# HGRN heads by tokens: scores as the stationary operand, squares summed on ScalarE, three transposes back to channels

## The chip, the cores and the metric

The program runs on one NeuronCore of a Trainium2 chip. The metric is the device time of one execution in microseconds (us); smaller is better. In this text PE is TensorE, DVE is VectorE, ACT is ScalarE, and POOL is GpSimd.

## The reference

One inference step of a two-layer trunk: layer 0 mixes tokens with an mLSTM, layer 1 with HGRN2, and each mixer is followed by a SwiGLU block. There are 256 prompt tokens and 8 sampled sequences of 8 tokens, so 320 tokens in all. The change touches only the HGRN2 mixer, whose core is, for each of 16 heads with 128 key channels and 128 value channels:

```python
def body(S, xs):
    qc, kc, lfc, ic = xs
    A = jnp.cumsum(lfc, axis=1)
    diff = jnp.where(causal[None, :, :, None, None], A[:, :, None] - A[:, None, :], -jnp.inf)
    wd = jnp.exp(diff)
    s = jnp.einsum('bthc,bjhc,btjhc->btjh', qc, kc, wd)
    oc = jnp.einsum('btjh,bjhv->bthv', s, ic) + jnp.einsum('bthc,bhcv->bthv', qc * jnp.exp(A), S)
    A_last = A[:, -1]
    S_new = jnp.exp(A_last)[..., None] * S + jnp.einsum('bjhc,bjhv->bhcv', kc * jnp.exp(A_last[:, None] - A), ic)
    return S_new, oc
...
o = rms_norm(from_chunks(os_), gn_g.reshape(H_HEADS, H_DV)).reshape(B, T, H_HEADS * H_DV)
out = (o * jax.nn.silu(g)) @ w_out.astype(jnp.float32)
```

The root mean square of `rms_norm` is taken for each token over the 128 value channels of a head.

## The kernel before

The activations are kept turned, channels on the 128 partitions and the 320 tokens along the free axis. Every weight matrix is read in tiles of 128 output columns by up to 16 blocks `k` of 128 rows. SP loads a tile (1 MB) into a ring of four slots `raw`. ACT copies it to `w_hi` in a rounded format (`split_high`, two halves), DVE subtracts to get the remainder `w_lo` (`split_low`, two halves), and PE makes three products for each k: hi by hi, hi by lo, lo by hi (`products`, lines 390 to 392), 48 products for a tile, each with 320 moving columns. `hi_done` counts ACT's halves, `lo_done` DVE's, `gemm_done` PE's tiles. Each engine has a program of its own in a fixed order written out by hand; semaphores alone tie them together.

The HGRN stage (`H_IN`) is a loop over 16 heads, four weight tiles a head: f, q, i, g. The work of a head is spread over three turns of the loop. In turn `it` PE makes the tiles of head `it`, and between them it does what belongs to the heads `one_back` and `two_back`:

- after tile 0: `h8(two_back)`, a product with a matrix of ones that sums the squares of the head's output over the channels (and spreads the sum over all partitions), and `turn_values(one_back)`, six transposes and one product;
- after tile 1: `by_columns(one_back)`, the many small products that give the scores, and last the old states' part of the sampled tokens, `OLD`;
- after tile 2: `h7(one_back)`, the head's outputs into `MX[5]` (bank 7), five products with the values `i_tok` as the stationary operand and the scores moving; the fifth adds `OLD`, which ACT copied to `hold_tok`. Then the products for the new states.

ACT squares the output (`h8`) when `h7` of PE is done (`g_o`), and in the next turn takes Ln and Exp of the sum (`h9`), which gives the reciprocal root `h_rs` of 128 by 320. DVE multiplies output, root and gate in `h9`, two passes, and `h10` of ACT and DVE round the result to `g_hi` and `g_lo`. At the end of each turn DVE copies the new prompt state (`prompt_S`), updates the eight sampled states (`sample_S`), and then makes `split_low` of the next head's tile 0, `h4` and `h5` (the keys and queries with their decays, up to `k_last` with `g_keys` at line 1379).

After the loop, the last two heads are finished within the first two tiles of the output projection `H_OUT` (`last_heads`): PE does `h8(14)` and `turn_values(15)` within tile 0, `by_columns(15)` within tile 1, then `h7(15)` and `h8(15)`, waits for `g_gated`, and makes the last two k of both tiles. Tile 2 of `H_OUT` is split by ACT only after the last states have been stored (`S_stored`).

Of the kernel before, what the change touches and what calls it, by code (L numbers as in the profile page):

```python
# [19 lines left out]
P = 128  # L20
D = 2048
KT = D // P
TP = 256
NB, TB = 8, 8
TS = NB * TB
T = TP + TS
# [3 lines left out]
HH = 16  # L30
# [65 lines left out]
def trunk(nc, x_prompt, x_sample, C_in, n_in, m_in, S_in, norm_mix_g, norm_ffn_g, norm_final_g,  # L96
# [7 lines left out]
    with ExitStack() as ctx:  # L104
# [148 lines left out]
        scores = carve(T)  # L253
# [8 lines left out]
        h_sq, h_rs = carve(T), carve(T)  # L262
        h_y = h_sq
        after_levels = Carve(at_pairs)
        i_half, hk_tok, hold_tok = after_levels(2 * P), after_levels(3, P), after_levels(P)
# [16 lines left out]
        I_TURNED, K_TURNED, OLD = bank[2][:, 0:3 * P], bank[3][:, 0:3 * P], bank[6][:, 3 * P:4 * P]  # L282
# [49 lines left out]
        g_gsig = sem("g_gsig")  # L332
# [4 lines left out]
        g_ikept, g_kkept, g_ihalf, g_o, g_sq, g_sum, g_rstd = (sem("g_" + n) for n in ("ikept", "kkept", "ihalf", "o", "sq", "sum", "rstd"))  # L337
# [287 lines left out]
        def _(act):  # L625
# [215 lines left out]
            def h7(h):  # L841
                act.wait_ge(g_levels, h + 1)
                act.activation(hold_tok, OLD, ACT.Copy)
                act.activation(hk_tok, K_TURNED.rearrange("p (a b) -> p a b", a=3), ACT.Copy).then_inc(g_kkept, 1)

            def h8(h):
                act.wait_ge(g_o, h + 1)
                act.activation(h_sq, MX[5][:, 0:T], ACT.Square).then_inc(g_sq, 1)

            def h9(h):  # L850
                act.wait_ge(g_sum, h + 1)
                act.activation(h_rs, MX[4][:, 0:T], ACT.Ln, scale=1.0 / P, bias=eps_col[:, :])
                act.drain()
                act.activation(h_rs, h_rs, ACT.Exp, scale=-0.5).then_inc(g_rstd, 1)
# [6 lines left out]
            def h_body(it, one_back, two_back):  # L861
# [10 lines left out]
                if two_back is not None:  # L872
                    h9(two_back)
# [19 lines left out]
            def h_end():  # L893
# [3 lines left out]
                h9(HH - 2)  # L897
# [6 lines left out]
                h9(HH - 1)  # L904
# [23 lines left out]
        def _(dve):  # L928
# [402 lines left out]
            def spread_near():  # L1331
# [7 lines left out]
                dve.copy_predicated(scores[:, TP:T].rearrange("p (j c) -> p j c", j=2), own_group[:, 0:2, :],  # L1339
                                    scores_near[:, 64:].rearrange("p (j c) -> p j c", j=1).to_broadcast((P, 2, 32)))  # L1340
# [76 lines left out]

            def h9(h):
                dve.wait_ge(g_rstd, h + 1)
                dve.tensor_tensor(h_y, MX[5][:, 0:T], h_rs, ALU.mult)  # L1420
                dve.drain()
                dve.tensor_tensor(h_y, h_y, gate, ALU.mult).then_inc(g_full, 1)
# [6 lines left out]
            def h_body(it, one_back, two_back):  # L1429
# [28 lines left out]
                if one_back is not None:  # L1458
                    prompt_S(one_back)
                    sample_S(one_back)  # L1460
                split_low(dve, H_IN, it + 1, 0)
# [13 lines left out]
            def h_end():  # L1475
# [10 lines left out]
                prompt_S(HH - 1)  # L1486
                h9(HH - 1)
# [17 lines left out]
        def _(pe):  # L1505
# [81 lines left out]

            picked = ident[:, :].rearrange("p (g r) -> p g r", g=4)[:, :, 0:PICKED]
# [165 lines left out]
            def h7(h):  # L1754
# [14 lines left out]
            def h8(h):  # L1769
                pe.wait_ge(g_sq, h + 1)  # L1770
                pe.wait_ge(g_Sp, h + 1)
                pe.matmul(MX[4][:, 0:T], ones[:, :], h_sq, start=True, stop=True).then_inc(g_sum, 1)  # L1772

            def h_body(it, one_back, two_back):
# [8 lines left out]
                if two_back is not None:  # L1783
                    pe.wait_ge(g_rstd, two_back + 1)
# [70 lines left out]
```

## Time and profile before

| | us |
|---|---|
| median of 3 runs | 3136.4 (3136.33, 3136.4, 3138.96) |
| profiled execution, its own time | 3136.22 |
| its span | 3134.7 |
| PE busy | 3082.4 (98%) |
| DVE busy | 1791.6 (57%) |
| ACT busy | 1169.5 (37%) |

The span is what the profile shows of the execution; what lies around it is 1.5 us. The busy time of an engine is the union of its instructions. The fp32 products that are not in the rounded format appear as two PE instructions each (two passes), the transposes as one.

### The profile page before, as it was taken

The page shows a single profiled execution, that of the slowest core. Times are in us where ns is not written, and L with a number is a line of the kernel's source. Part 1 is how long each engine was busy: PE and PEld are TensorE (multiplying, and loading weights), DVE is VectorE, ACT ScalarE, POOL GpSimd, SP SyncE. Part 2 cuts the span into 40 slices and gives each one's busy share as a digit, 9 for nine tenths or more (in the row PEclk, how much of TensorE's full clock was granted, in tenths as well). Part 3 has the DMA queues.
Part 4 walks back from the last instruction along what each step waited for, and adds up shares of the span by engine and source line. Part 5 has one row for each costly group of instructions (what it writes and reads, how often), then busy time and mean ns, then how long its engine had stood idle before and what let it go on. Part 6 is the DMA issues. An engine that isn't in the chain of part 4 may idle for free.

```text
span 3134.7 us, 58211 instructions
## 1 busy us (share of the span) xinstructions
PE 3082.4 (98%) x23124; PEld 3037.3 (97%) x23124; DVE 1791.6 (57%) x3128; ACT 1169.5 (37%) x1658; POOL 74.4 (2%) x132
## 2 busy tenths in 40 slices
PE   7999999999999999999999999989999999999998
PEld 6999989999999999999999999989999999999997
DVE  6666665555445544555687888755555345544554
ACT  4433333333223332334455555534333233322333
POOL 2000000000000000000000000000000000000000
PEclk9999999999999999999999999989999999999999
DMA  6564636555555555555555565545555555555543
GB/s 158 149 190 136 191 111 184 146 152 147 148 148 148 151 154 150 148 141 141 159 159 160 141 167 156 149 127 150 148 147 150 153 145 153 149 149 148 147 134 114
DMA packets 856561, 470.15 MB, mean 150 GB/s; under 512 B 10424, under 2 KB 846144, under 8 KB 856480
## 3 DMA queue, kind: packets, MB, share of 16 engines
q1 hardware_dynamic: 844080, 433.09, 50.2%
q0 software_dynamic: 10144, 35.74, 3.7%
q8 instruction: 57, 0.93, 0.1%
q10 hardware_dynamic: 2256, 0.19, 0.1%
q14 instruction: 24, 0.20, 0.0%
HBM read 447.46 MB, written 21.53 MB: 150 GB/s over the span
## 4 chain that ended last, share of the span: by engine, by line
PE 97%; DVE 1%; DMA 1%; ACT 0%; issue 0%; DVEq 0%; ACTq 0%; POOL 0%; POOLq 0%
PE bank L390 31%; PE bank L392 30%; PE bank L391 30%; PE bank L1718 1%; DMA arena<-in_mlstm_w_in_dram 0%; PE bank L1766 0%; PE bank L1772 0%; PE bank L1610 0%; PE bank L1764 0%; PE bank L1561 0%; PE bank L1599 0%; PE bank L1750 0%; PE bank L1592 0%; PE bank L1630 0%; DVE w_lo L380 0%
## 5 line engine op out<-in xcount | busy, mean ns | idle before, releaser
L390 PE MATMUL bank<-h_hi,w_hi 128*128 128x320 f32 x4608 | 1433.5, 311 | 5.8 <-DVE w_lo L380 4.9
L391 PE MATMUL bank<-h_lo,w_hi 128*128 128x320 f32 x4608 | 1424.5, 309 | 0.1
L392 PE MATMUL bank<-h_hi,w_lo 128*128 128x320 f32 x4608 | 1424.5, 309 | 0.0
L373 ACT ACTIVATE w_hi<-raw 128x1024 fp32r<-128x1024 f32 (+1 forms) x832 | 818.8, 1032 | 778.1 <-PE bank L392 774.6
L380 DVE TENSOR_TENSOR w_lo<-raw,w_hi 128x1024 fp32r<-128x1024 f32 (+1 forms) x832 | 963.3, 1199 | 199.3 <-ACT w_hi L373 198.6
L390 PEld LDWEIGHTS bank<-h_hi,w_hi 128*128 128x128 f32 x4608 | 865.8, 188 | 22.7 <-issue 16.6
L391 PEld LDWEIGHTS bank<-h_lo,w_hi 128*128 128x128 f32 x4608 | 866.0, 188 | 1.6 <-issue 1.3
L392 PEld LDWEIGHTS bank<-h_hi,w_lo 128*128 128x128 f32 x4608 | 865.7, 188 | 0.0
L390 PE MATMUL bank<-g_hi,w_hi 128*128 128x320 f32 x1920 | 598.5, 312 | 14.0 <-DVE w_lo L380 6.4
L391 PE MATMUL bank<-g_lo,w_hi 128*128 128x320 f32 x1920 | 596.2, 311 | 0.0
L392 PE MATMUL bank<-g_hi,w_lo 128*128 128x320 f32 x1920 | 596.2, 310 | 0.0
L1054 DVE TENSOR_TENSOR arena<-bank,rstd 128x320 f32<-128x320 f32 (+1 forms) x296 | 133.6, 460 | 532.0 <-PE bank L392 515.4
L390 PEld LDWEIGHTS bank<-g_hi,w_hi 128*128 128x128 f32 x1920 | 363.2, 189 | 16.3 <-DVE w_lo L380 7.3
L391 PEld LDWEIGHTS bank<-g_lo,w_hi 128*128 128x128 f32 x1920 | 363.3, 189 | 0.0
L392 PEld LDWEIGHTS bank<-g_hi,w_lo 128*128 128x128 f32 x1920 | 363.1, 189 | 0.0
L1212 DVE TENSOR_TENSOR x<-x,bank 128x320 f32 (+1 forms) x128 | 62.3, 487 | 316.1 <-PE bank L392 316.0
L782 ACT ACTIVATE arena<-arena 128x320 f32<-128x320 f32 x88 | 41.5, 472 | 482.3 <-DVEq L1248 482.3
L413 ACT ACTIVATE h_hi<-x,gains (+1 forms) x48 | 27.0, 563 | 189.7 <-DVEq L1217 182.3
L423 DVE SCALAR_TENSOR_TENSOR h_lo<-x,gains,h_hi (+1 forms) x48 | 26.5, 552 | 53.2 <-ACT h_hi L413 53.2
L1254 DVE TENSOR_TENSOR g_hi<-arena 128x320 f32 (+1 forms) x88 | 43.3, 493 | 14.7 <-issue 13.8
L1258 DVE TENSOR_TENSOR g_lo<-arena,g_hi 128x320 f32 (+1 forms) x88 | 43.3, 492 | 12.5 <-issue 11.6
L417 ACT ACTIVATE arena<-x 128x320 f32 (+1 forms) x64 | 29.4, 459 | 54.8 <-DVEq L1217 54.8
(318 smaller groups left out, 1446.8 us busy)
## 6 DMA issues: line engine op xcount, KB each, us to landing
raw<-in_ffn_w_up_dram SPq DMA_DIRECT2D x176, 1024.0 KB, 5.7
raw<-in_ffn_w_down_dram SPq DMA_DIRECT2D x64, 1024.0 KB, 5.8
raw<-in_hgrn_w_in_dram SPq DMA_DIRECT2D x64, 1024.0 KB, 6.3
raw<-in_mlstm_w_in_dram SPq DMA_DIRECT2D x48, 1024.0 KB, 6.1
raw<-in_ffn_w_down_dram SPq DMA_DIRECT2D x32, 768.0 KB, 5.0
raw<-in_mlstm_w_out_dram SPq DMA_DIRECT2D x16, 1024.0 KB, 6.0
raw<-in_hgrn_w_out_dram SPq DMA_DIRECT2D x16, 1024.0 KB, 5.8
raw<-in_state_mlstm_C_dram POOLq DMA_DIRECT2D x8, 1024.0 KB, 9.1
```

The lines of the kernel that those rows point to most:

```text
L373: act.activation(w_hi[:, s % 2, part], raw[:, s % ph.ring, part], ACT.Copy).then_inc(hi_done, 1)
L380: dve.tensor_tensor(w_lo[:, s % 2, part], raw[:, s % ph.ring, part], w_hi[:, s % 2, part].bitcast(F32), ALU.subtract).then_inc(lo_done, 1)
L390: pe.matmul(out, tile_hi, hi[:, k, :], start=(k == 0), stop=False)
L391: pe.matmul(out, tile_hi, lo[:, k, :], start=False, stop=False)
L392: last = pe.matmul(out, tile_lo, hi[:, k, :], start=False, stop=(k == ph.k - 1))
L417: act.activation(square[:, parity, :], x[:, bass.ds(j, 1), :], ACT.Square).then_inc(x_sq_done, 1)
L782: act.activation(f_sig[:, (s - 1) // 2, :], fa[:, (s - 1) // 2, :], ACT.Sigmoid).then_inc(f_sig_done, 1)
L1054: return dve.tensor_tensor(out, src, rstd[:, cols], ALU.mult)
L1212: add = dve.tensor_tensor(x[:, bass.ds(j, 1), :], x[:, bass.ds(j, 1), :], bank[s % ph.banks][:, 0:T].rearrange("p (a t) -> p a t", a=1), A ...
L1254: dve.tensor_tensor(g_hi[:, bass.ds(pair, 1), :], f_sig[:, u:u + 1, :], fu.rearrange("p (a t) -> p a t", a=1), ALU.mult)
L1258: dve.tensor_tensor(g_lo[:, bass.ds(pair, 1), :], f_full[:, u:u + 1, :], g_hi[:, bass.ds(pair, 1), :].bitcast(F32), ALU.subtract).then_inc ...
L1718: last = pe.matmul(LEVEL[li][group(j), 32 * b:32 * b + 32], left[:, c], right[:, c], start=True, stop=True)
```

## The change

The outputs are made with tokens on the partitions: in PE's `h7` the scores are now the stationary operand and the values move. `OLD` is written straight into the third block of the output bank, so the fifth product, ACT's copy to `hold_tok` and that buffer are gone; the sampled tokens' scores are laid out in 128 columns instead of 64, with the 64 tokens in groups of 16. ACT squares each of three blocks of 128 by 128 and sums it along the free axis into one word (`accum_out`), and takes Ln and Exp of 128 by 3 words in the same turn; DVE scales the three blocks by them (`scale_out`) into `o_tok`. PE turns the three blocks back to channels in place of the product with ones, the third with the columns of the identity permuted so that the tokens come out in order. DVE's `h9` multiplies only by the gate. PE no longer waits for `g_rstd` ahead of `by_columns`.

```diff
-        scores = carve(T)
+        scores = carve(TP + P)
...
-        I_TURNED, K_TURNED, OLD = bank[2][:, 0:3 * P], bank[3][:, 0:3 * P], bank[6][:, 3 * P:4 * P]
+        I_TURNED, K_TURNED, OLD = bank[2][:, 0:3 * P], bank[3][:, 0:3 * P], bank[7][:, 2 * P:3 * P]
...
             def h7(h):
                 act.wait_ge(g_levels, h + 1)
-                act.activation(hold_tok, OLD, ACT.Copy)
                 act.activation(hk_tok, K_TURNED.rearrange("p (a b) -> p a b", a=3), ACT.Copy).then_inc(g_kkept, 1)
 
             def h8(h):
                 act.wait_ge(g_o, h + 1)
-                act.activation(h_sq, MX[5][:, 0:T], ACT.Square).then_inc(g_sq, 1)
-
-            def h9(h):
-                act.wait_ge(g_sum, h + 1)
-                act.activation(h_rs, MX[4][:, 0:T], ACT.Ln, scale=1.0 / P, bias=eps_col[:, :])
+                for b in range(3):
+                    act.activation(o_tok[:, b, :], MX[5][:, b * P:(b + 1) * P], ACT.Square, accum_out=o_sums[:, b:b + 1])
                 act.drain()
-                act.activation(h_rs, h_rs, ACT.Exp, scale=-0.5).then_inc(g_rstd, 1)
+                act.activation(o_rs, o_sums, ACT.Ln, scale=1.0 / P, bias=eps_col[:, :])
+                act.drain()
+                act.activation(o_rs, o_rs, ACT.Exp, scale=-0.5).then_inc(g_rstd, 1)
...
+            def scale_out(h):
+                dve.wait_ge(g_rstd, h + 1)
+                dve.tensor_tensor(o_tok, MX[5][:, 0:3 * P].rearrange("p (b c) -> p b c", b=3),
+                                  o_rs.rearrange("p (b c) -> p b c", c=1).to_broadcast((P, 3, P)), ALU.mult).then_inc(g_scaled, 1)
+
             def h9(h):
-                dve.wait_ge(g_rstd, h + 1)
-                dve.tensor_tensor(h_y, MX[5][:, 0:T], h_rs, ALU.mult)
-                dve.drain()
-                dve.tensor_tensor(h_y, h_y, gate, ALU.mult).then_inc(g_full, 1)
+                dve.wait_ge(g_oturned, h + 1)
+                dve.tensor_tensor(h_y, MX[4][:, 0:T], gate, ALU.mult).then_inc(g_full, 1)
...
                     prompt_S(one_back)
                     sample_S(one_back)
+                    scale_out(one_back)
                 split_low(dve, H_IN, it + 1, 0)
                 h4(it)
...
-                pe.matmul(out[:, 0:P], i_tok[:, 0, :], scores[:, 0:P], start=True, stop=True, skip_group_check=True)
-                pe.matmul(out[:, P:TP], i_tok[:, 1, :], scores[:, P:TP], start=False, stop=True, skip_group_check=True)
-                pe.matmul(out[:, P:TP], i_tok[:, 0, :], scores_far, start=False, stop=True, skip_group_check=True)
-                pe.matmul(out[:, TP:T], i_tok[:, 2, :], scores[:, TP:T], start=False, stop=True, skip_group_check=True)
-                pe.matmul(out[:, TP:T], hold_tok, picked, start=False, stop=True, skip_group_check=True)
+                pe.matmul(out[:, 0:P], scores[:, 0:P], i_tok[:, 0, :], start=False, stop=True, skip_group_check=True)
+                pe.matmul(out[:, P:TP], scores[:, P:TP], i_tok[:, 1, :], start=False, stop=False, skip_group_check=True)
+                pe.matmul(out[:, P:TP], scores_far, i_tok[:, 0, :], start=False, stop=True, skip_group_check=True)
+                pe.matmul(out[:, TP:TP + P], scores[:, TP:], i_tok[:, 2, :], start=False, stop=True, skip_group_check=True)
...
             def h8(h):
-                pe.wait_ge(g_sq, h + 1)
+                pe.wait_ge(g_scaled, h + 1)
                 pe.wait_ge(g_Sp, h + 1)
-                pe.matmul(MX[4][:, 0:T], ones[:, :], h_sq, start=True, stop=True).then_inc(g_sum, 1)
+                for b in range(2):
+                    pe.transpose(MX[4][:, b * P:(b + 1) * P], o_tok[:, b, :], ident[:, :])
+                pe.transpose(MX[4][:, TP:TP + P].rearrange("p (u g r) -> p u g r", u=2, g=4), o_tok[:, 2, :], picked_first).then_inc(g_oturned, 1)
```

PE's program between tile 0 and the six transposes of `turn_values`, in the loop's body, before (L1772 is the product with ones, L1725 the first of `turn_values`):

```order
L392 MATMUL bank<-h_hi,w_lo 128x320
L1770 REGISTER_ALU
L1772 MATMUL bank<-arena,ones 128x320 [waits g_Sp,g_sq]
L1722 ISA
L1725 MATMUL bank<-ident,arena 128x128 [waits g_S,evac_done]
```

and with the change (its L1728 is the line that was L1725):

```order
L392 MATMUL bank<-h_hi,w_lo 128x320
L1772 REGISTER_ALU
L1775 MATMUL bank<-ident,arena 128x128 [waits g_Sp,g_scaled]
L1775 MATMUL bank<-ident,arena 128x128
L1776 MATMUL bank<-ident,arena 128x128
L1725 ISA
L1728 MATMUL bank<-ident,arena 128x128 [waits g_S,evac_done]
```

One product of 320 columns became three transposes of 128 columns, and it waits for a result of DVE instead of one of ACT.

PE's `h7` in the loop's body before, with the two products for the prompt state (L1764) behind it:

```order
L1758 MATMUL bank<-arena 128x128 [waits g_kkept,g_ihalf,g_full]
L1759 MATMUL bank<-arena 128x128
L1760 MATMUL bank<-arena 128x128
L1761 MATMUL bank<-arena 128x64
L1762 MATMUL bank<-ident,arena 128x64
L1764 MATMUL bank<-arena 128x128 x2
```

and with the change:

```order
L1761 MATMUL bank<-arena 128x128 [waits g_kkept,g_ihalf,g_full]
L1762 MATMUL bank<-arena 128x128
L1763 MATMUL bank<-arena 128x128
L1764 MATMUL bank<-arena 128x128
L1766 MATMUL bank<-arena 128x128 x2
```

Two products of 64 columns became one of 128; the waits are the same.

DVE's program at the end of a turn before, from `sample_S` (L1414) to the split of the next head's tile 0 (L380):

```order
L1407 COPY arena<-bank 128x128 [waits S_stored]
L1414 SCALAR_TENSOR_TENSOR arena<-arena,bank 128x128 x8
L379 ISA
L380 TENSOR_TENSOR w_lo<-raw,w_hi 128x1024 [waits hi_done]
```

and with the change:

```order
L1402 COPY arena<-bank 128x128 [waits S_stored]
L1409 SCALAR_TENSOR_TENSOR arena<-arena,bank 128x128 x8
L1417 TENSOR_TENSOR arena<-bank,arena 128x384 [waits g_rstd]
L379 ISA
L380 TENSOR_TENSOR w_lo<-raw,w_hi 128x1024 [waits hi_done]
```

`scale_out`, with its wait for ACT, now stands ahead of the split; its own two passes in `h9` became one.

## Rows read from the trace of the kernel before

**Rows 1.** The page, busy time, share of the span, instructions:

```profile
PE 3082.4 (98%) x23124; PEld 3037.3 (97%) x23124; DVE 1791.6 (57%) x3128; ACT 1169.5 (37%) x1658; POOL 74.4 (2%) x132
```

**Rows 2.** Windows, one turn of the loop; PEclk is the granted clock:

```profile
core 0: us, PE busy (x) PEld busy (x) DVE busy (x) ACT busy (x) POOL busy (x), PEclk, DMA share, GB/s
1781.00:1815.15 34.15, 34.15 (x370) 33.10 (x369) 27.52 (x73) 17.84 (x34) 2.34 (x3) 1.00 0.56 155
```

**Rows 3.** Timeline of PE between tiles 0 and 1 (start us, length us):

```profile
1780.85 0.70 PE L1772 MATMUL bank<-arena,ones 128*128 128x320 f32 x2
1781.39 0.49 PE L1725 MATMUL bank<-ident,arena 128*128 128x128 f32 x3
1781.72 0.49 PE L1728 MATMUL bank<-ident,arena 128*128 128x128 f32 x3
...
1782.42 0.31 PE L391 MATMUL bank<-h_lo,w_hi 128*128 128x320 f32 x1
```

**Rows 4.** Timeline of PE, start of tile 2 and `h7`:

```profile
1791.38 0.41 PE L390 MATMUL bank<-h_hi,w_hi 128*128 128x320 f32 x1
...
1798.53 0.38 PE L1758 MATMUL bank<-arena 128*128 128x128 f32 x2
...
1799.19 0.33 PE L1761 MATMUL bank<-arena 128*128 128x64 f32 x2
1799.36 0.39 PE L1762 MATMUL bank<-ident,arena 128*128 128x64 f32 x2
1799.58 0.66 PE L1764 MATMUL bank<-arena 128*128 128x128 f32 x4
```

**Rows 5.** Timeline of PE's weight loads in the same `h7`:

```profile
1799.08 0.30 PEld L1761 LDWEIGHTS bank<-arena 128*128 128x128 f32 x2
1799.30 0.30 PEld L1762 LDWEIGHTS bank<-ident,arena 128*128 128x128 f32 x2
1799.53 0.53 PEld L1764 LDWEIGHTS bank<-arena 128*128 128x128 f32 x4
```

**Rows 6.** Line 1728, transposes of `turn_values`, duration min/median/max in ns:

```profile
L1728 PE MATMUL bank<-ident,arena x48: 272/273/328, 1541.3 to 2050.8; 128*128 128x128 f32 x48
```

**Rows 7.** Timeline of DVE, end of a turn and the next turn's first split:

```profile
1801.26 2.15 DVE L1414 SCALAR_TENSOR_TENSOR arena<-arena,bank 128x128 f32<-128x128 f32 x8
1803.32 2.35 DVE L380 TENSOR_TENSOR w_lo<-raw,w_hi 128x1024 fp32r<-128x1024 f32 x2
...
1813.77 2.35 DVE L380 TENSOR_TENSOR w_lo<-raw,w_hi 128x1024 fp32r<-128x1024 f32 x2
```

**Rows 8.** Timeline of ACT, reads of a bank in the loop:

```profile
1791.51 0.28 ACT L843 ACTIVATE arena<-bank 128x128 f32<-128x128 f32 x1 [3.19 <-PE bank L1750]
1791.68 0.49 ACT L844 ACTIVATE arena<-bank 128x384 f32<-128x384 f32 x1
...
1800.96 0.44 ACT L848 ACTIVATE arena<-bank 128x320 f32<-128x320 f32 x1 [5.11 <-PE bank L1766]
```

**Rows 9.** Timeline of ACT, a square's sum being read out at the start:

```profile
30.22 0.20 ACT L649 ACTIVATION_READ_ACCUMULATOR g_lo<-arena 64x1 f32 x1
30.32 0.52 ACT L637 ACTIVATE h_hi<-bank,gains 128x320 fp32r<-128x320 f32 x1
```

**Rows 10.** Groups of ACT's instructions in the last 16 us (count, busy us, mean ns):

```profile
L916 ACT ACTIVATE rstd_cols<-bank,eps_col 128x2 f32<-128x2 f32 (+1 forms) x2 | 0.4, 254 | 0.0
L919 ACT ACTIVATE rstd_cols<-rstd_cols 128x2 f32<-128x2 f32 (+1 forms) x2 | 0.3, 194 | 0.1
```

**Rows 11.** Waits of PE from 2030 to 2090 us (total us, times, longest):

```profile
PE bank L390 <- DVE w_lo L380: 6.4, 1, 6.4
PE bank L390 <- DVE g_lo L1426: 3.4, 1, 3.4
PE bank L1758 <- DVE arena L1401: 1.2, 1, 1.2
PE bank L1772 <- ACT arena L848: 0.6, 1, 0.6
PE bank L1728 <- DVE arena L1379: 0.3, 1, 0.3
```

**Rows 12.** Timelines of PE, DVE and ACT behind the last `h7`:

```profile
2050.52 0.55 PE L1728 MATMUL bank<-ident,arena 128*128 128x128 f32 x3 [0.25 <-DVE arena L1379]
...
2067.46 0.44 ACT L848 ACTIVATE arena<-bank 128x320 f32<-128x320 f32 x1 [6.74 <-PE bank L1766]
...
2070.45 0.49 DVE L1422 TENSOR_TENSOR arena<-arena 128x320 f32<-128x320 f32 x1
```

**Rows 13.** Windows around PE's restart at tile 2 of `H_OUT`:

```profile
2084.00:2086.00 2.00, 2.00 (x9) 2.00 (x8) 1.28 (x3) 2.00 (x4) 0.00 (x0) 0.50 0.55 144
2088.00:2090.00 2.00, 2.00 (x16) 2.00 (x15) 0.03 (x1) 0.00 (x0) 0.00 (x0) 1.00 0.44 104
```

More of the change, by code:

```diff
@@ L261, in trunk @@
         gate = carve(T)
-        h_sq, h_rs = carve(T), carve(T)
-        h_y = h_sq
+        h_y, o_tok = carve(T), carve(3, P)
+        o_sums, o_rs = carve(3), carve(3)
         after_levels = Carve(at_pairs)
-        i_half, hk_tok, hold_tok = after_levels(2 * P), after_levels(3, P), after_levels(P)
+        i_half, hk_tok = after_levels(2 * P), after_levels(3, P)
         assert after_levels.at <= at_pairs + sum(level_width(l) for l in LEVELS)
@@ L329, in trunk @@
         n_turned, n_done, n_stored = sem("n_turned"), sem("n_done"), sem("n_stored")
-        g_gsig = sem("g_gsig")
+        g_gsig, g_scaled = sem("g_gsig"), sem("g_scaled")
         g_fsig, g_f, g_logf = sem("g_fsig"), sem("g_f"), sem("g_logf")
@@ L336, in trunk @@
         g_pair, g_keys, g_turned, g_levels = sem("g_pair"), sem("g_keys"), sem("g_turned"), sem("g_levels")
-        g_ikept, g_kkept, g_ihalf, g_o, g_sq, g_sum, g_rstd = (sem("g_" + n) for n in ("ikept", "kkept", "ihalf", "o", "sq", "sum", "rstd"))
+        g_ikept, g_kkept, g_ihalf, g_o, g_rstd, g_oturned = (sem("g_" + n) for n in ("ikept", "kkept", "ihalf", "o", "rstd", "oturned"))
         g_Sp = sem("g_Sp")
@@ L871, in h_body @@
                     h6(one_back)
-                if two_back is not None:
-                    h9(two_back)
                 split_high(act, H_IN, it, 2)
@@ L896, in h_end @@
                 h6(HH - 1)
-                h9(HH - 2)
                 act.wait_ge(evac_done, H_IN.end)
@@ L903, in h_end @@
                 h8(HH - 1)
-                h9(HH - 1)
                 h10(HH - 1)
@@ L1338, in spread_near @@
                                     scores_near[:, 0:64].rearrange("p (b j c) -> p b j c", b=2, j=1).to_broadcast(shape))
-                dve.copy_predicated(scores[:, TP:T].rearrange("p (j c) -> p j c", j=2), own_group[:, 0:2, :],
-                                    scores_near[:, 64:].rearrange("p (j c) -> p j c", j=1).to_broadcast((P, 2, 32)))
+                dve.copy_predicated(scores[:, TP:].rearrange("p (j u w) -> p j u w", j=2, u=2)[:, :, :, 0:PICKED],
+                                    own_group[:, 0:2, :].rearrange("p j (u r) -> p j u r", u=2),
+                                    scores_near[:, 64:].rearrange("p (j u r) -> p j u r", j=1, u=2).to_broadcast((P, 2, 2, PICKED)))
             def h3(h):
@@ L1486, in h_end @@
                 prompt_S(HH - 1)
+                scale_out(HH - 1)
                 h9(HH - 1)
@@ L1586, in m4 @@
                 pe.matmul(MX[0][:, TP + P:TP + P + TS], kT[:, TP:TW], qT[:, TP:T], start=True, stop=True).then_inc(m_scores, 1)
+            picked_first = ident[:, :].rearrange("p (g u r) -> p u g r", g=4, u=2)
             picked = ident[:, :].rearrange("p (g r) -> p g r", g=4)[:, :, 0:PICKED]
@@ L1782, in h_body @@
                 products(pe, H_IN, it, 1, h_hi, h_lo)
-                if two_back is not None:
-                    pe.wait_ge(g_rstd, two_back + 1)
                 if one_back is not None:
@@ L1806, in last_heads @@
                 if at == (1, 6):
-                    pe.wait_ge(g_rstd, HH - 1)
                     by_columns(HH - 1)
```

## The prediction

> **What bounds the kernel now.** I read the page first: PE is busy 98% of the span, DVE 57%, ACT 37% [rows 1]. The windows of the HGRN loop come next. One turn takes 34.15 us, PE is busy for all of it at full clock, DVE for 27.52 and ACT for 17.84 [rows 2], and the waits of PE over seven turns in a row list nothing. So inside the loop a change of PE's own instructions shows in the time one for one, and work on DVE or ACT is free until it is late for PE. Behind the loop it is the other way round: PE waits there for 0.3, 1.2, 0.6, 3.4 and 6.4 us [rows 11], and the chain through ACT and DVE counts. The kernel is therefore summed in two parts: the loop, up to the moment at which head 14's `h7` is done (`g_o`), by PE's instructions; behind that, by the chain.
>
> **Part one, the product with ones becomes three transposes.** The timeline gives starts, and in a stream it is the distance of starts that costs. From L1772 to L1725 there are 0.54 us (two passes of 320 columns, 0.27 each). From the first L1725 to the first L1728 there are 0.33 us for three transposes, 0.11 each, with other transposes behind them [rows 3]. The new instructions have that shape and stand right ahead of these. To L391 at 1782.42 the stretch from L1725 is 1.03 us, so nothing is hidden at its end. I take 0.54 - 0.33 = 0.21 off, and 0.20 because the seven loads ahead of tile 1 go at 0.11 each and the first may not be covered by a long product any more. The third transpose reads the identity in another order; the fifth product of `h7` reads it in pieces of 16 already and shows the pace of its neighbours (0.22 for two passes, 1799.36 to 1799.58 [rows 4]), so I give that nothing. Bounds: 0.22 saved; or, if each transpose costs its recorded duration of 273 ns [rows 6], 0.82 - 0.54 = 0.28 lost.
>
> **Part two, `h7`.** Moving columns are 128+128+128+64+64 = 512 before and 4 x 128 = 512 after, so by columns nothing is saved. But the two products of 64 columns do not cost half: from 1799.19 to 1799.58 they take 0.39 us, while the three of 128 ahead of them take 0.66, 0.22 each [rows 4]. The reason stands in the weight loads: a pair of passes starts its loads every 0.22 us, whatever the columns (1799.08, 1799.30, 1799.53 [rows 5]). One stationary operand less, with two loads, is 0.22. From the starts of the products it is 0.39 - 0.22 = 0.17. I take 0.22, since the loads set the pace and the product at L1764 can start no earlier than its own load; bounds 0 and 0.22. Changing which operand is stationary costs nothing by these rows: both are 128x128 words.
>
> The Trainium skill ("TensorE: Matmul & The Clock Gate", Part 2, "LDWEIGHTS (loading the stationary operand)") says that a load lasts its number of columns over 1.2 GHz, 107 ns for 128, whatever the rows; the trace agrees with 0.11 us of pitch, and by it two loads less are 0.21 in place of 0.22.
>
> **Sum of the loop.** `h7` of heads 0 to 14 lies ahead of the cut: 15 x 0.22 = 3.3 us. `h8` of heads 0 to 13 too: 14 x 0.20 = 2.8. Together 6.1 us less.
>
> **What the loop hides.** ACT's copy to `hold_tok` goes (0.17 of pitch [rows 8]); it had no reader that was late. ACT's `h8` grows. A square of 128x128 from a bank is 0.28 long and 0.17 in pitch [rows 8], and each sum is read out by an instruction of 0.20, 0.10 in pitch [rows 9]: three are 3 x 0.27 + 0.10 = 0.91 us, at most 3 x 0.48 = 1.44. Ln and Exp of three words are like the small ones at the end, 0.25 and 0.19 [rows 10], with some 0.07 for each drain: 1.49 in all, 2.1 at most. From 1800.96 [rows 8] the root is there at 1802.5, or 1803.1. DVE comes to `scale_out` when `sample_S` is done, at 1803.3 [rows 7]: it does not wait. `scale_out` is 384 columns from a bank; at 0.49 for 320 [rows 12] that is 0.58 long, and since successive passes overlap by about 0.1, 0.47 of delay. Behind it on DVE stand the split of the next tile 0, `h4`, `h5` and the split of tile 1. Tile 0's first half is ready at 1803.32 + 1.14 = 1804.5, later 1804.9; PE needs it when tile 3 ends, some 7.1 us before L1772 of the next turn, which starts at 1780.85 + 34.15 = 1815.0 (a tile lasts 1798.53 - 1791.38 = 7.15 [rows 4]), so at 1807.9: 3 us in hand. Tile 1's first half is ready at 1813.77 + 1.14 = 1814.9 [rows 7], later 1815.4; PE starts tile 1 one product before the L391 of [rows 3] plus 34.15, at 1816.4, and 0.2 sooner by the shorter `h8`: 0.8 us in hand. This is the thinnest cover of the change: 0.47 of 1.5 us is used. ACT starts its split of tile 0 one us later and still feeds DVE in time (first half done 1803.5). DVE gives the 0.4 back when `h9` makes one pass in place of two. The removed wait of PE for `g_rstd` was not felt, and its removal is worth nothing.
>
> **Part three, the end.** Counted from `g_o` of head 14, DVE is 0.47 later at `g_keys`, for which PE already waits 0.25 us [rows 11, 12], because in `last_heads` only five k stand in place of a whole tile. So the 0.20 that `h8(14)` saves turns into waiting, and the rest of the chain (`by_columns(15)`, then DVE's level work, for which PE waits 1.2) moves by +0.47. `h7(15)` gives 0.22 back. Then the last output: from ACT's square at 2067.46 to the end of DVE's second pass at 2070.45 + 0.49 = 2070.94 there are 3.48 us [rows 12]. In their place: ACT 1.49, DVE 0.58, three transposes after a wait 0.55 [rows 12], DVE's gate 0.49, and 0.03 for each of three hand-overs: 3.20, so -0.28 (up to +0.3 with the dear squares). The rounding to `g_hi`, `g_lo`, the states and their store behind it are unchanged. Net: +0.47 - 0.22 - 0.28 = 0.0.
>
> **Total:** -6.1 us. Against the profiled execution, 3136.22, that is 3130.1; against the median of the runs shown, 3136.4, which lies 0.2 above it, 3130.3. I give **3130.2 us**. What a measurement of this kernel can tell from no change is about 0.2%, 6.3 us, so the forecast sits right at that bound, just inside "no change".
>
> [...] The trace shows the transposes of `turn_values` at a pitch of 0.11 us inside a turn whose clock is granted in full [rows 2, 3]. [...]
>
> **Rivals.**
> - *Transposes in series.* Each costs its duration [rows 6]: +0.28 x 14 = +3.9 in the loop, -3.3 from `h7`: 3136.9. Against it is the pitch of six of them [rows 3]; for it only that no transposes follow a product of the rounded format now. 4 in 100.
> - *Columns, not loads, set `h7`.* The new fourth product costs 0.39 with what it replaces: only 2.8 is saved, 3133.4. The 0.22 of load pitch speaks against it. With the half-way case of 0.17 (3131.0), 14 in 100 lie between 3131.0 and 3133.6.
> - *PE's clock behind the loop.* After its 6.4 us wait PE runs at 1.2 GHz (0.50 in the windows at 2084) and is back at 2.4 GHz by 2088 [rows 13]; nine products in 2 us there against sixteen later. These some 6 us cost about 2.6. Since all of it now comes 6 us sooner, the clock may come back sooner or later after the restart: I allow -1.5 to +1.5, 3128.7 or 3131.7. 8 in 100 for each side beyond the forecast's own range.
> - *Slower: the root is late for DVE, and DVE for tile 1.* `scale_out` waits for ACT ahead of the split, so a late root holds DVE, and PE pays once the cover of 1.5 us is used. Each turn already has 0.42 to give. To end over 3142.7 the wait of PE has to be 0.42 + 0.45 = 0.87 in each of 14 turns, so DVE has to be late by about 1.3 + 0.87 = 2.1 us in place of 0.47; the root would then come at about 1805, four us after `g_o`, against an upper bound of 2.1. With twice the bound, 3143. 5 in 100.
>
> **How the numbers follow.** The forecast, 3129.2 to 3131.0, has 58 in 100; the series 4, the columns 14, the clock 8 and 8, the slower one 5, and 3 remain for what I do not see. The range from 3127.4 to 3133.6 leaves out the series, the slower case, the rest and a little of the clock. Faster by over 0.2% means below 3130.1: half of the forecast's case (0.29), the sooner clock (0.08), and what I do not see (0.03), together 0.40. Slower by over 0.2% is the last rival, 0.05. The other half of the forecast, the series, the columns and the later clock stay within: 0.55.
>
> **What the profile would show.** A turn of 33.73 us in place of 34.15, with PE busy throughout; three new transposes with starts 0.11 apart; four pairs of passes in `h7` 0.22 apart; no wait of DVE at `scale_out`; PE's wait for `g_keys` of head 15 grown from 0.3 to about 0.9; the wait ahead of the last products about as before. Wrong would be: a wait of PE on `w_lo` inside the loop, a pitch of the transposes above 0.15, or a last output that takes over a us more.

## The result and the profile after

| | before | changed |
|---|---|---|
| median, 10 runs each | 3138.46 us (3136.33 to 3139.63) | 3131.27 us (3128.51 to 3135.28) |
| ratio | | 0.9979, 95% interval 0.9970 to 0.9987 |
| profiled execution, own time | 3136.22 us | 3131.71 us |
| its span | 3134.7 us | 3130.1 us |

The kernel became faster by 0.21%, 6.6 us by the ratio, and the interval (4.1 to 9.4 us) excludes no change. It lies right at the 0.2% that the prediction took as the least that can be told from no change. The forecast was 6.2 us less. The medians are 7.2 us apart, the two profiled executions only 4.5; most of that gap stands ahead of the HGRN stage, where the two kernels do the same, and is told below.

The page after, busy time, share and instructions, against [rows 1]:

```profile
PE 3078.0 (98%) x23108; PEld 3035.7 (97%) x23108; DVE 1789.3 (57%) x3128; ACT 1168.5 (37%) x1722; POOL 74.4 (2%) x132
```

PE lost 4.4 us of busy time, and ACT has 64 instructions more (for each of 16 heads two more squares and three readings of sums, less one copy) in the same time. The windows of one turn of the loop after, against [rows 2]:

```profile
core 0: us, PE busy (x) PEld busy (x) DVE busy (x) ACT busy (x) POOL busy (x), PEclk, DMA share, GB/s
1824.08:1857.80 33.72, 33.72 (x376) 32.87 (x371) 27.41 (x72) 17.85 (x38) 2.34 (x3) 1.00 0.57 158
```

A turn takes 33.72 us in place of 34.15, and PE is still busy for all of it. The timeline of PE after, between tiles 0 and 1 (start us, length us), against [rows 3]:

```profile
1814.16 0.38 PE L1775 MATMUL bank<-ident,arena 128*128 128x128 f32 x2
1814.38 0.27 PE L1776 MATMUL bank<-ident,arena 128*128 128x128 f32 x1
1814.49 0.49 PE L1728 MATMUL bank<-ident,arena 128*128 128x128 f32 x3
1814.82 0.49 PE L1731 MATMUL bank<-ident,arena 128*128 128x128 f32 x3
```

The three new transposes take 1814.49 - 1814.16 = 0.33 us, where the product with ones took 0.54. The third one, with the identity in another order, costs 0.11 like the others. The same view at `h7`, against [rows 4]:

```profile
1831.62 0.38 PE L1761 MATMUL bank<-arena 128*128 128x128 f32 x2
1831.84 0.39 PE L1762 MATMUL bank<-arena 128*128 128x128 f32 x2
1832.06 0.39 PE L1763 MATMUL bank<-arena 128*128 128x128 f32 x2
1832.29 0.39 PE L1764 MATMUL bank<-arena 128*128 128x128 f32 x2
1832.51 0.61 PE L1766 MATMUL bank<-arena 128*128 128x128 f32 x4
```

Four products at 0.22 each, 0.89 us, where five took 1.05. The state products behind them last 0.61 where they lasted 0.66: that is the other 0.05 of the 0.22 that the prediction took from the starts of the weight loads. ACT and DVE at the end of the turn, against [rows 7, 8]:

```profile
1833.83 0.28 ACT L848 ACTIVATE arena<-bank 128x128 f32<-128x128 f32 x1 [5.05 <-PE bank L1768]
1834.01 0.20 ACT L848 ACTIVATION_READ_ACCUMULATOR arena<-bank 128x1 f32 x1
...
1834.79 0.30 ACT L850 ACTIVATE arena<-arena,eps_col 128x3 f32<-128x3 f32 x1
1835.15 0.21 ACT L852 ACTIVATE arena<-arena 128x3 f32<-128x3 f32 x1
```

```profile
1834.13 2.15 DVE L1409 SCALAR_TENSOR_TENSOR arena<-arena,bank 128x128 f32<-128x128 f32 x8
1836.19 0.55 DVE L1417 TENSOR_TENSOR arena<-bank,arena 128x384 f32<-128x384 f32 x1
1836.66 2.35 DVE L380 TENSOR_TENSOR w_lo<-raw,w_hi 128x1024 fp32r<-128x1024 f32 x2
```

The root is there at 1835.36, 1.53 us after the first square began (1.49 was reckoned), and DVE comes to `scale_out` (L1417) at 1836.19 without a wait. It delays the split by 0.47. Behind the loop, the waits of PE from 2020 to 2090 us, against [rows 11]:

```profile
PE bank L390 <- DVE w_lo L380: 6.5, 1, 6.5
PE bank L1775 <- DVE arena L1417: 2.2, 1, 2.2
PE bank L390 <- DVE g_lo L1426: 1.7, 1, 1.7
PE bank L1761 <- DVE arena L1396: 1.2, 1, 1.2
PE bank L1731 <- DVE arena L1374: 0.9, 1, 0.9
```

The wait for the keys of head 15 (L1374) is 0.9 us in place of 0.3, as forecast. The product with ones stood between two waits of 0.6 and 3.4; now the transposes stand between 2.2 and 1.7.

From one event to the next, the pair of profiled executions differs like this (us, after less before):

| stretch | before | after | difference |
|---|---|---|---|
| start to the old states' products of head 0 | 1550.57 | 1552.51 | +1.94 |
| to the same of head 1 | 35.15 | 35.16 | 0.0 |
| 13 more turns, to head 14 | 444.34 | 438.71 | -5.63 |
| to ACT's first square of head 14 | 9.97 | 9.75 | -0.22 |
| to PE's restart at tile 2 of the output projection | 42.09 | 42.09 | 0.0 |
| to the end of the span | 1052.6 | 1051.9 | -0.7 |

The first and the last row can't be put down to the change. Both kernels do the same work ahead of head 0's old states' products and behind the restart, and a second profiled execution of the same changed kernel (run a2, below) has 1552.7 us in the first row and 1052.8 in the last, which is 0.2 more than before; its row of 42.09 and its steady turn of 33.72 are the same. The first two turns vary as well: together they take 69.65 us before and 69.93 in e10, a variant of before with an edit behind the loop only, and 69.28 and 68.62 in the two executions of the changed kernel.

### The profile page after: what moved, and what is told of

Its sections match the earlier page's. It is cut to its first block, busy times and chain, and to the rows that moved or that the text cites. A ratio compares the mean times of both kernels' runs of the same rounds, so it can differ in the third digit from the quotient of the medians.

```text
span 3130.1 us, 58228 instructions
## 1 busy us (share of the span) xinstructions
PE 3078.0 (98%) x23108; PEld 3035.7 (97%) x23108; DVE 1789.3 (57%) x3128; ACT 1168.5 (37%) x1722; POOL 74.4 (2%) x132
## 4 chain that ended last, share of the span: by engine, by line
PE 97%; DVE 1%; DMA 1%; ACT 0%; issue 0%; DVEq 0%; ACTq 0%; POOL 0%; POOLq 0%
PE bank L390 31%; PE bank L392 30%; PE bank L391 30%; PE bank L1721 1%; DMA arena<-in_mlstm_w_in_dram 0%; PE bank L1768 0%; PE bank L1613 0%; DMA out_dram<-arena 0%; PE bank L1563 0%; PE bank L1602 0%; PE bank L1753 0%; PE bank L1595 0%; PE bank L1766 0%; DVE w_lo L380 0%; PE bank L1633 0%
## 5 line engine op out<-in xcount | busy, mean ns | idle before, releaser
L380 DVE TENSOR_TENSOR w_lo<-raw,w_hi 128x1024 fp32r<-128x1024 f32 (+1 forms) x832 | 964.0, 1201 | 198.5 <-ACT w_hi L373 198.1
L1048 DVE TENSOR_TENSOR arena<-bank,rstd 128x320 f32<-128x320 f32 (+1 forms) x296 | 133.9, 462 | 532.5 <-PE bank L392 515.8
```

The costliest lines, as they stand in the source:

```text
L380: dve.tensor_tensor(w_lo[:, s % 2, part], raw[:, s % ph.ring, part], w_hi[:, s % 2, part].bitcast(F32), ALU.subtract).then_inc(lo_done, 1)
L1048: return dve.tensor_tensor(out, src, rstd[:, cols], ALU.mult)
```

## The experiments

Times of a turn are read from the chain of each profiled execution, as the distance of the same product in two neighbouring turns. Every experiment from e1 to e7 and e11 was run once. These are the rows of the changed kernel (start us, length us), then of e1, e2, e3 and e6:

```profile
1824.08 0.46 PE bank L1753 x15
1857.80 0.46 PE bank L1753 x15
```

```profile
1825.99 0.46 PE bank L1753 x15
1859.93 0.46 PE bank L1753 x15
```

```profile
1823.60 0.46 PE bank L1753 x15
1857.32 0.46 PE bank L1753 x15
```

```profile
1826.53 0.46 PE bank L1753 x15
1860.58 0.46 PE bank L1753 x15
```

```profile
1825.74 0.46 PE bank L1750 x15
1859.65 0.46 PE bank L1750 x15
```

So 33.72, 33.94, 33.72, 34.05 and 33.91 us. The times of one kernel spread over 4.3 us (before, 21 runs) to 6.8 us (changed, 10 runs), so for an effect of 0.2 us a turn it is these rows that decide and not the total.

**e1, one stationary operand more, the same columns.**

```diff
-                pe.matmul(out[:, TP:TP + P], scores[:, TP:], i_tok[:, 2, :], start=False, stop=True, skip_group_check=True)
+                for half in range(2):
+                    c = slice(64 * half, 64 * half + 64)
+                    pe.matmul(out[:, TP + 64 * half:TP + 64 * half + 64], scores[:, TP:], i_tok[:, 2, c], start=False, stop=True, skip_group_check=True)
```

> The changed kernel with the fourth product of h7 made as two of 64 moving columns with the same stationary scores: the same columns, one stationary operand (two loads) more. My theory, that weight loads set the pace of these products at 0.11 us each: a turn of 33.72 + 0.17 to 0.22 = 33.89 to 33.94 us. The rival, that moving columns set it: 33.72.

Measured: 33.94, which is 0.22 more. The moving columns are the same 128, so columns can't be the cause. By their starts the products themselves go from 0.22 to 0.39 us, and the state products behind them from 0.54 to 0.60, as in the kernel before.

**e2, half of the columns, the same stationary operands.**

```diff
-                pe.matmul(out[:, 0:P], scores[:, 0:P], i_tok[:, 0, :], start=False, stop=True, skip_group_check=True)
+                pe.matmul(out[:, 0:64], scores[:, 0:P], i_tok[:, 0, 0:64], start=False, stop=True, skip_group_check=True)
```

and the other three likewise.

> The changed kernel with only the first 64 value channels computed in all four products of h7 (half of the moving columns, the same stationary operands; the outputs of the other channels are left out). Loads set the pace: from the first of the four to the state products still about 0.8 to 0.9 us, a turn of 33.6 to 33.72. Columns set the pace: 0.45 us, a turn of 33.28.

Measured: 33.72, unchanged to the hundredth. The timeline of PE in this run:

```profile
1831.14 0.33 PE L1761 MATMUL bank<-arena 128*128 128x64 f32 x2
1831.31 0.39 PE L1762 MATMUL bank<-arena 128*128 128x64 f32 x2
1831.53 0.39 PE L1763 MATMUL bank<-arena 128*128 128x64 f32 x2
1831.75 0.39 PE L1764 MATMUL bank<-arena 128*128 128x64 f32 x2
1831.98 0.66 PE L1766 MATMUL bank<-arena 128*128 128x128 f32 x4
```

The first pair looks 0.05 shorter by its start, and the state products behind give it back (0.66 in place of 0.61). That is what made the removed pair of the kernel before look like 0.17 in the starts, where 0.22 was saved. The two limits meet near 128 columns: a pass of 320 columns costs 0.27 us [rows 3], so 128 of them are, by an estimate from that row, 0.108 us, and a load is 0.11. Below 128 columns only the load is left, and 64 columns cost what 128 do.

**e3, the transposes as ordinary products.**

```diff
-                    pe.transpose(MX[4][:, b * P:(b + 1) * P], o_tok[:, b, :], ident[:, :])
+                    pe.matmul(MX[4][:, b * P:(b + 1) * P], o_tok[:, b, :], ident[:, :], start=True, stop=True)
```

and the third likewise.

> The changed kernel with the three transposes of h8 made as ordinary products with the identity, two passes each. My theory, that a transpose is one pass at a pitch of 0.11 us and that PE bounds the loop: 0.66 in place of 0.33 us, a turn of 34.05 us, and behind the loop at most 0.3 more. If the transposes went in series with their duration of 0.27, two passes would add 0.8 or more.

Measured: 34.05, 0.33 more: three passes more at 0.11. In these traces a transpose of fp32 words is one pass and a product two, and that is what makes the part pay (0.66 would be dearer than the product with ones, 0.54).

**e6, the two parts apart, on the kernel before.**

```diff
-                pe.matmul(out[:, TP:T], hold_tok, picked, start=False, stop=True, skip_group_check=True)
```

> The kernel before without the fifth product of h7 (the old states' part of the sampled tokens' outputs is left out); ACT's copy of it stays. It separates the two parts of the change: my theory gives h7 0.22 of the 0.43 us of a turn, so 34.15 - 0.22 = 33.93 us here, and the other 0.21 is the transposes' in place of the product with ones. The rival: the removed product is worth its 64 columns in two passes, 0.05, and the rest of the gain came from elsewhere: 34.10.

Measured: 33.91, against 34.15. That product alone is worth 0.24 us a turn. With the 0.21 that the rows give for the transposes (0.54 less 0.33) it makes 0.45, where 0.43 was measured: the two parts add up within 0.02.

**e4 and e5, more work for DVE.** On the changed kernel one pass more of DVE in e4 and three in e5, whose edit is:

```diff
                     scale_out(one_back)
+                    for _ in range(3):
+                        dve.tensor_tensor(h_y, gate, gate, ALU.mult)
+                        dve.drain()
```

> The changed kernel with one more pass of DVE over 320 columns and a drain behind scale_out in the loop, some 0.57 us. By the trace after, tile 1's first half is ready 1.0 us before PE starts tile 1, so no wait: a turn of 33.72 us; behind the loop PE's wait for the keys of head 15 grows from 0.92 to about 1.5 us. The rival, that DVE is already felt by PE: a turn longer by up to 0.57.

> The same with three such passes, some 1.7 us in all, more than the cover of 1.0. PE should wait for the low half of tile 1 by about 0.7 us in each turn: 34.4 us, the whole execution some 10 us longer than the changed kernel (0.7 x 13 and 1.7 less 0 behind the loop). If the cover is larger than I read, less.

e4: a turn from 1824.98 to 1858.70, 33.72 us, so nothing is felt. Behind the loop the wait for the keys grew to 1.22 and not to 1.5: ahead of L1048 behind the loop DVE paused for 0.23 us there where it pauses for 0.61 in the changed kernel, so that pause swallowed some of the delay (more on it under e7). e5: 34.85 us, and 34.86 in the turns behind, so 1.14 more where 0.7 was expected; 3150.9 us in all, 19.6 more than the changed kernel where 10 were expected. From the chain of this run, with PE's wait in the timeline:

```profile
1832.66 1.08 PE bank L1724 x93
1867.51 1.08 PE bank L1724 x93
```

```profile
1824.92 0.41 PE L390 MATMUL bank<-h_hi,w_hi 128*128 128x320 f32 x1 [0.87 <-DVE w_lo L380]
```

The wait is where it was said to be, at the first product of tile 1 for its low half. The profile calls 0.87 us of it a wait; by the starts that product comes 1.25 us behind the one ahead of it (1823.67), in the changed kernel 0.14. It is longer than expected because DVE reaches the split of tile 1 later by 2.04 us and not by 1.7: from the copy of the state to that split it takes 14.92 us (1808.73 to 1823.65), in the changed kernel 12.88 (1833.92 to 1846.80). The three passes and their drains are 1.79 of it, and 0.25 are longer pauses of DVE behind them, for which the profile names no cause. 2.04 - 1.14 gives the cover that was left: 0.90 us, with 0.8 forecast. So `scale_out` used a third of a cover of 1.4 (0.47 + 0.90), and 0.9 us more on DVE before the split of tile 1 would have been free.

**e7 and e11, the delay of the keys behind the loop.** `scale_out` behind the keys, in the loop and for head 14 behind it, and `h8(14)` behind `turn_values(15)`:

```diff
                 dve.tensor_scalar(k_last, k0[:, 0:P], e(2), e(3), ALU.mult, ALU.mult).then_inc(g_keys, 1)
+                if scaled is not None:
+                    scale_out(scaled)
                 pair_diffs(h, 1)
...
-                    scale_out(one_back)
                 split_low(dve, H_IN, it + 1, 0)
...
                 if at == (0, 5):
-                    h8(HH - 2)
                     turn_values(HH - 1)
+                    h8(HH - 2)
```

> The changed kernel with scale_out of DVE moved behind the keys (g_keys) of the next turn, and, for the last heads, PE's turn_values(15) ahead of h8(14). Loop unchanged at 33.72 us a turn. Behind it the wait for the keys of head 15 shrinks again: from ACT's square of head 14 to PE's restart at tile 2 of the output projection 42.09 - 0.47 = 41.6 us. If it was not scale_out that made the keys late there, 42.09.

The loop stayed at 33.72, but the stretch behind it is 42.12 us (2036.77 to 2078.89), not 41.6. The theory that the late keys cost 0.47 there fell as it stood. From ACT's square of head 14 to the end of the keys it is 10.40 us, and 10.90 in the changed kernel. That is 0.50 less, close to the 0.47 that was expected, but it isn't what `scale_out` cost. DVE in the changed kernel, and then in e7:

```profile
2038.96 2.35 DVE L380 TENSOR_TENSOR w_lo<-raw,w_hi 128x1024 fp32r<-128x1024 f32 x2
2045.62 0.49 DVE L1048 TENSOR_TENSOR arena<-bank,rstd 128x320 f32<-128x320 f32 x1 [0.61 <-issue]
```

```profile
2039.45 2.36 DVE L380 TENSOR_TENSOR w_lo<-raw,w_hi 128x1024 fp32r<-128x1024 f32 x2 [0.23 <-ACT w_hi L373]
2045.74 0.49 DVE L1048 TENSOR_TENSOR arena<-bank,rstd 128x320 f32<-128x320 f32 x1 [0.24 <-issue]
```

Counted from the square (2036.13 and 2036.77), the split (L380) starts after 2.83 us in the changed kernel and after 2.68 in e7: only 0.15 sooner, because with `scale_out` out of the way DVE waits for ACT, whose longer `h8` stands ahead of its own half of the split. Another 0.37 comes from the pause ahead of L1048. It is 0.61 us in nine of the profiled executions, and 0.23 or 0.24 in the five (e4, e5, e7, e11, e12) in which DVE's program of the loop was edited; why, no run shows. Before and changed kernel both have the 0.61, so between these two the 0.47 stands: the split starts 2.36 us behind the square before, and 2.83 after.

PE gained nothing from the sooner keys. Its `h8(14)` used to lie in the wait for them, and in e7 it lies behind it and costs its 0.33; what is left, 0.13, went to a wait for the low part of tile 1, of which PE wants both halves here, and for which DVE was as late as before, since `scale_out` now stands between the keys and that split: PE's first product of the tile starts at 2052.30, 0.05 after the end of the split (2049.90 + 2.35). The same 0.05 stands in the changed kernel (2051.70 behind 2049.29 + 2.36) and 0.06 before (2055.14 behind 2052.73 + 2.35), so keys and split hold PE there in one, and to bring the keys alone forward gains nothing. To see whether that reading holds, `scale_out(14)` goes behind the split of tile 1 and `h8(14)` into that tile:

```diff
                 h5(HH - 1)
                 split_low(dve, H_OUT, 0, 1)
+                scale_out(HH - 2)
...
                 if at == (0, 5):
                     turn_values(HH - 1)
+                if at == (1, 3):
+                    h8(HH - 2)
```

> As e7, but behind the loop scale_out(14) stands also behind DVE's split of tile 1 of the output projection, and PE makes h8(14) only at k = 3 of that tile. In e7 the keys came 0.50 us sooner, and nothing was gained, because h8(14), 0.33 us, left PE's waiting time, and by my reading 0.13 more went to a wait for tile 1's low half. So from ACT's square of head 14 to that of head 15: 27.67 - 0.50 + 0.33 = 27.50 us here, 27.63 if tile 1's half was not what held e7.

Measured: 2036.30 to 2063.81, 27.51 us, as expected for the reading that the low part of tile 1 held e7 (27.50). So the edits are worth 0.16 us in all. The keys are as early as in e7, and by the same two parts, so this 0.16 holds for a kernel with the short pause; what the order alone is worth was not measured.

**e8 and e10, the wait of 6.5 us.** The waits of PE show something as large as the change: behind the last output PE waits 6.4 us in both kernels [rows 11], because ACT splits tile 2 only after the states have been stored, and DVE after the residual tile that waits for the same. The edit, for the output projection alone, on ACT and on DVE (on DVE too the splits of tiles 2 and 3 leave their old place):

```diff
-                    if not (ph is H_OUT and s < 2):
+                    if ph is not H_OUT:
                         split_high(act, ph, 0, s)
                     if s in boundary:
                         boundary[s]()
+                    if ph is H_OUT and s in (1, 2):
+                        split_high(act, ph, 0, s + 1)
                     if s == 1 and ph is H_OUT:
                         act.wait_ge(S_stored, HH * 32)
...
                     dve.sem_inc(x_done, 1)
+                    if between:
+                        between()
                     x_tile_dve(dve, r, j, s % 2, isinstance(j, int) and j == 0)
...
+                        early = ph is H_OUT and s < 3
+                        x_evac(ph, r, 0, s - 1, (lambda: split_low(dve, ph, 0, s + 1)) if early else None)
```

> The changed kernel with the splits of tiles 2 and 3 of the output projection made by ACT and DVE ahead of the wait for the stored states instead of behind it. The wait of 6.5 us of PE for w_lo there falls to about 1 us, so 5.5 us less; PE's clock, low from 2068 on, should come back sooner by as much. I expect 3126 us or less beside 3131 for the changed kernel, ratio to the kernel before 0.996. The rival: tile 3 or the residual tiles behind it become late instead, and part of it is given back.

Measured: 3123.18 us (3122.72 to 3125.04, 4 runs), ratio to before 0.9954, interval 0.9938 to 0.9971. The timeline of PE, with its last two waits:

```profile
2065.66 0.64 PE L390 MATMUL bank<-g_hi,w_hi 128*128 128x320 f32 x1 [1.70 <-DVE g_lo L1431]
2070.10 0.64 PE L390 MATMUL bank<-g_hi,w_hi 128*128 128x320 f32 x1 [0.87 <-DVE w_lo L380]
```

and the windows behind it, in which the number behind the six busy times is the granted clock (0.50, then 0.98):

```profile
2070.00:2074.00 4.00, 3.90 (x15) 3.90 (x15) 1.65 (x4) 1.07 (x3) 0.00 (x0) 0.50 0.73 196
2074.00:2078.00 4.00, 4.00 (x28) 4.00 (x28) 3.75 (x7) 2.57 (x4) 0.00 (x0) 0.98 0.66 193
```

The wait fell from 6.46 to 0.87, and PE is at 2.4 GHz again some 4 us after the restart, which is within what the other executions show (3.0 to 6.2 us).

> The kernel before with the splits of tiles 2 and 3 of the output projection ahead of the wait for the stored states, as in the run e8. The wait of 6.4 us is the same in both kernels, so the same 5.6 us should go, and the ratio to before be 0.9975 to 0.998; together with the change's 0.998 that would make up the ratio of e8, 0.9954. If the two shared one gain, e10 would come out near e8.

e10: 3130.39 us (10 runs), ratio 0.9977, interval 0.9968 to 0.9986; its wait for w_lo is 1.0 us. 0.9977 x 0.9979 = 0.9956, and e8 has 0.9954: the two gains are apart. e10 gained 8 us by the medians where the wait gave 5.4. Its trace has 6.2 us less from ACT's square of head 14 to the restart (35.92 in place of 42.09), of which 0.7 is the clock: the twelve products ahead of the wait take 2.8 us there, with the clock full at their start, and 3.6 before, all at 0.50. In e8 they run at 0.50 as well, and it has 5.56 less (36.53). For the rest of the 8 us the intervals are too wide.

**a2 and e12.** The changed kernel again, and e12, both on the chip of e10.

> The changed kernel again, unedited, beside the kernel before on one chip, to have it timed together with the two kernels below. 6 to 7 us less than before by the turns of the loop (0.43 x 14 and nothing gained or lost behind it): ratio 0.998. If what PE's clock does at the restarts were part of the gain, the ratio would differ from 0.998 by more than 0.0005.

> The edits of e8 and e11 together on the changed kernel. About 0.2 us less than e8 by the chain, which timing can't tell; so a ratio to before of 0.995 to 0.9955, and about 6 us less than the changed kernel on the same chip. Against: the two edits meet on DVE in the first two tiles of the output projection, and one may take back what the other gives; then 0.996.

| | median | runs | ratio to before | interval |
|---|---|---|---|---|
| before | 3138.40 | 21 | | |
| a2, the changed kernel | 3131.80 | 11 | 0.9978 | 0.9969 to 0.9987 |
| e10, before with the early splits | 3130.39 | 10 | 0.9977 | 0.9968 to 0.9986 |
| e12, change, early splits and e11's order | 3125.84 | 5 | 0.9961 | 0.9947 to 0.9974 |

The change's ratio came out the same a second time. e12 beats before, a2 and e10: all of its five times, 3123.56 to 3126.32, lie below theirs. Its ratio missed the expected 0.995 to 0.9955 and came out at the 0.996 of the rival, but its interval holds both, and the trace doesn't bear the rival out: from square to square of heads 14 and 15 it has 27.51 us, as e11, where e8 has 27.67. It then loses more than that, 36.68 us to the restart in place of 36.53, because its clock was at 0.50 already in the transposes of head 15 (0.64 long, 0.44 in e8). Against a2 it is 6.0 us less, as expected. It isn't told apart from e8.

## Why the prediction was right

- **PE bounds the loop; its instructions show one for one.** Shown: the turn went from 34.15 to 33.72 (33.73 forecast) with PE busy throughout, and e1, e3 and e6 moved it by the passes that they added or removed, to 0.02.
- **Transposes for the product with ones, 0.20.** 0.21 by the rows after, and e3 shows that it rests on the single pass. The rival of transposes in series is out: it stood on the duration of 273 ns, which the new ones have too (272), while their starts are 0.11 apart.
- **`h7`, 0.22 by loads and not 0.17 or 0 by columns.** e1 and e2 settle it from both sides; e6 gives 0.24 on the kernel before. The rival of the columns is out.
- **The root in time for DVE, cover of 0.8 at tile 1.** Root after 1.53 us (1.49 forecast), no wait; e5 measures the cover as 0.90. The slower rival was far off: DVE would have had to be late by 0.90 + 0.87 us more than it was.
- **Behind the loop, +0.47 - 0.22 - 0.28 = 0.0.** The total is right, 42.09 in both kernels. By its terms: from square to square of heads 14 and 15 it is 27.43 before and 27.67 after, +0.24 where +0.25 was forecast; from the square to the end of DVE's gate 3.48 and 3.24, -0.24 with -0.28 forecast. The +0.47 itself is seen where DVE starts the split. e7 shows that a later `scale_out` would not save it: ACT, with its longer `h8`, would give DVE its half only 0.15 sooner, and `h8(14)`, 0.33, lies hidden in the wait. The prediction said that ACT still feeds DVE in time, which is so, but with 0.15 us to spare and no more.
- **The sum.** -5.63 - 0.22 = -5.85 in the loop, with -6.1 forecast; the steady turns have their 0.43 each, and the missing 0.25 lies in the first two. In the second execution (a2) the same stretch is 6.5 shorter than before, so these 0.25 lie within the spread of those turns, and no term of the sum is shown to be off by them. The ratio of all runs gives -6.6, and its interval holds all of these.
- **The clock.** The rival was that the clock comes back sooner or later at the restart because all of it comes sooner. In the pair of executions it did: 3.7 us at 1.2 GHz behind the restart where it was 5.8 before. But in a2, the same changed kernel, it was 6.2 us. The windows of the first execution, then of a2:

```profile
2080.00:2082.00 2.00, 2.00 (x9) 2.00 (x9) 1.18 (x3) 2.00 (x4) 0.00 (x0) 0.52 0.48 123
2082.00:2084.00 2.00, 2.00 (x16) 2.00 (x15) 2.00 (x2) 0.70 (x1) 0.00 (x0) 1.00 1.11 321
```

```profile
2082.00:2084.00 2.00, 2.00 (x9) 2.00 (x9) 1.70 (x2) 0.25 (x1) 0.00 (x0) 0.51 1.10 315
2084.00:2086.00 2.00, 2.00 (x16) 2.00 (x15) 0.00 (x0) 0.00 (x0) 0.00 (x0) 1.00 0.33 81
```

PE restarted at 2078.22 and at 2077.78. Over the 14 profiled executions the clock came back after 3.0 to 6.2 us, so the -0.7 at the end of the table is one draw from a spread, and no run shows that the change moved it. The allowance of 1.5 us either way covers it: from the restart to the end the 14 executions take 1051.7 to 1052.8 us. The clock moved more at the start (below).

The 3136.4 of the runs shown was the lower end of what the kernel before does: 21 more runs lie from 3136.04 to 3140.38. So the time, 3131.27, came out 1.1 over the forecast while the gain by the ratio was 0.4 more. That puts it 0.3 above the 3129.2 to 3131.0 in which the prediction saw its own case, and among the times that it gave to the columns; that case is out by e1 and e2, and the reason is the starting point, which three runs had put 2 us too low.

## What to carry to other kernels

Where products in fp32 have 128 columns or fewer (64 and 128 were measured), count the stationary operands and not the moving columns: each pass cost a load of 0.11 us here, so two narrow products merged into one of double width were a gain of a whole pair of passes. Price a matmul in a stream by the distance of starts, never by its duration, and look one row further, since a start can borrow 0.05 us that the next group gives back. When an engine off the path gets work ahead of a buffer that the busy engine needs, read the cover before every such buffer in turn; and a wait that grows may be one in which useful work lies hidden, so removing its cause frees only the difference. Before a stretch of two profiled executions is explained, compare it in two executions of one kernel: here that took away the clock's part.

## What the runs showed of the hardware that was not expected

The times of the kernel before spread from 3136.0 to 3140.4 us, and its profiled execution, 3136.22, was at the lower end. The granted clock at the start of the program goes with it. In the profiled execution of before it is full from 28 to 42 us, in that of the changed kernel it is not, though both kernels are the same there (windows, the changed kernel first):

```profile
28.00:36.00 8.00, 5.32 (x20) 4.57 (x21) 4.74 (x8) 4.08 (x8) 0.98 (x1) 0.66 0.29 78
36.00:42.00 6.00, 6.00 (x36) 5.35 (x34) 2.90 (x9) 1.06 (x2) 0.00 (x0) 0.89 0.81 248
```

```profile
28.00:36.00 8.00, 5.32 (x33) 4.50 (x33) 5.08 (x9) 4.42 (x10) 0.98 (x1) 1.00 0.25 58
36.00:42.00 6.00, 6.00 (x40) 5.52 (x41) 4.20 (x11) 3.19 (x5) 0.00 (x0) 1.00 0.88 274
```

PE is busy for the same 5.32 us of the first window and gets through 20 matmuls instead of 33. Three of the 14 profiled executions (before, e8, e12) had the full clock there and reached the old states' products of head 0 between 1550.1 and 1550.4 us by the timeline of PE; the eleven others had 0.57 to 0.79 in the first window and reached them between 1551.8 and 1553.3. That is the +1.94 us of the table. It hides three tenths of the gain when these two profiles are compared: 4.5 us are seen, and 6.5 without it. What decides in an execution whether the clock falls there was not tried; the transfers of the two executions differ there too (0.29 and 0.25 of the DMA engines' time in the first window).

The reading of a sum that `accum_out` adds cost 0.20 us in duration, 0.09 between starts; three squares with their readings took 0.88 us (1833.83 to 1834.71) where one square of 320 columns took 0.44 [rows 8].
